# Reordered work at the layer boundaries of a two-block network kernel

## The reference

```python
mem_n = rmsnorm(mem, mem_norm_g)
for i in range(2):
    mem_k, mem_v = split(mem_n @ mem_w_kv[i])
    x = x + 0.5 * swiglu(rmsnorm(x, norm_g[i, 0]), ffn_w_up[i, 0], ffn_w_down[i, 0])
    h = rmsnorm(x, norm_g[i, 1])
    mix = pool_layer(h, ..., mem_k, mem_v) if i == 0 else diff_layer(h, ..., mem_k, mem_v)
    x = x + mix
    x = x + 0.5 * swiglu(rmsnorm(x, norm_g[i, 2]), ffn_w_up[i, 1], ffn_w_down[i, 1])
x = rmsnorm(x, final_norm_g)
```

```python
mod = silu(c) @ w_ada + b_ada            # 1024 x 6144 weights
x = x + g1 * hybrid_mixer(modulate(rms_norm(x), sh1, sc1), w_in, w_out, rel_bias)
x = x + g2 * peer_ffn(modulate(rms_norm(x), sh2, sc2), wq, subkeys, u_emb, v_emb)
```

## Time and profile before

| | us |
|---|---|
| three runs | 1996.73, 2003.67, 2005.41 |
| median | 2003.67 |
| span of the profiled execution | 1999.3 |
| PE busy in it | 1767.5 |
| DVE busy | 1275.6 |
| ACT busy | 795.6 |

### The profile page before, as it was taken

The page is one execution under the profiler, slowest core; times in us unless marked ns, Lnnn a source line. Parts: engine busy times, 40 slices in busy tenths (PEclk is TensorE's granted clock), DMA queues, the critical chain, the costliest instruction groups (busy, mean ns, idle before and its releaser), DMA issues.

```text
span 1999.3 us, 22974 instructions
## 1 busy us (share of the span) xinstructions
PE 1767.5 (88%) x8110; PEld 1301.8 (65%) x8110; DVE 1275.6 (64%) x2212; ACT 795.6 (40%) x1423; POOL 651.7 (33%) x602
## 2 busy tenths in 40 slices
PE   7999999999999999999999789759987787777786
PEld 6877898887888778978888788645533233333332
DVE  4567766665465556765654676478687888864554
ACT  5444435544354435575443456422222222321111
POOL 4453450144114451111444112023433334333330
PEclk9999999999999999999999799879999989899988
DMA  8999986799799989858999564378999999999995
GB/s 259 330 366 388 300 274 226 264 337 366 281 321 332 378 307 341 296 206 293 323 377 328 192 203 162 106 294 344 391 419 420 419 419 421 419 420 421 420 420 221
DMA packets 247275, 650.00 MB, mean 325 GB/s; under 512 B 14945, under 2 KB 156562, under 8 KB 214418
## 3 DMA queue, kind: packets, MB, share of 16 engines
q1 hardware_dynamic: 200210, 346.15, 50.4%
q0 software_dynamic: 46304, 301.52, 37.8%
q10 hardware_dynamic: 672, 1.18, 0.2%
HBM read 643.56 MB, written 139.48 MB: 392 GB/s over the span
## 4 chain that ended last, share of the span: by engine, by line
PE 44%; DMA 33%; POOL 9%; DVE 7%; issue 3%; ACT 3%; SPq 0%; ACTq 0%; DVEq 0%; POOLq 0%
DMA late_uv<-uv_rows,M 15%; DMA adaW<-in_w_ada 11%; PE P L1256 8%; DMA early_uv<-uv_rows,M 4%; PE P L719 3%; PE P L721 3%; PE P L720 3%; POOL adaW L556 3%; PE PX L802 3%; PE PX L804 3%; PE PX L803 3%; POOL adaW L557 2%; PE P L668 2%; POOL adaW L558 2%; PE P L669 2%
## 5 line engine op out<-in xcount | busy, mean ns | idle before, releaser
L1778 DVE TENSOR_TENSOR WL<-WR,WH 128x1024 fp32r<-128x1024 f32 (+1 forms) x246 | 323.8, 1357 | 203.4 <-ACT WH L1301 203.2
L1301 ACT ACTIVATE WH<-WR 128x1024 fp32r<-128x1024 f32 (+1 forms) x272 | 271.0, 1044 | 342.7 <-PE P L721 143.2
L1256 PE MATMUL P<-early_uv,M 128*128 128x512 f32 x576 | 280.8, 645 | 85.5 <-ACT M L1712 85.5
L802 PE MATMUL PX<-WH,hTh 128*128 128x512 f32 x704 | 280.6, 399 | 6.8 <-DVE WL L1786 4.5
L804 PE MATMUL PX<-WH,hTl 128*128 128x512 f32 x704 | 275.9, 392 | 0.0
L1256 PEld LDWEIGHTS P<-early_uv,M 128*128 128x128 f32 x576 | 115.6, 206 | 245.3 <-issue 141.0
L803 PE MATMUL PX<-WL,hTh 128*128 128x512 f32 x704 | 275.0, 391 | 0.0
L1256 PE MATMUL P<-late_uv,M 128*128 128x512 f32 x448 | 219.9, 648 | 60.3 <-ACT M L1712 60.3
L1793 DVE TENSOR_TENSOR WL<-WR,WH 128x1024 fp32r<-128x1024 f32 x128 | 179.2, 1440 | 136.9 <-ACT WH L1310 136.9
L653 POOL DMA_INDIRECT early_uv<-uv_rows,M x144 | 139.9, 972 | 302.2 <-PE P L1256 183.7
L2362 DVE CUSTOM_DVE_ANT_0 early_uv<-early_uv,PX 128x1024 f32<-128x1024 f32 x144 | 172.0, 1219 | 92.6 <-DMA early_uv<-uv_rows,M 92.2
(11 more groups left out here) (365 smaller groups left out, 3166.1 us busy)
## 6 DMA issues: line engine op xcount, KB each, us to landing
WR<-in_ffn_w_up SPq DMA_DIRECT2D x88, 1024.0 KB, 10.0
WR<-in_ffn_w_down SPq DMA_DIRECT2D x44, 1024.0 KB, 11.1
uv_rows<-in_peer_u SPq DMA_DIRECT2D x35, 1024.0 KB, 13.5
uv_rows<-in_peer_v SPq DMA_DIRECT2D x35, 1024.0 KB, 14.4
uv_rows<-in_peer_u SPq DMA_DIRECT2D x58, 512.0 KB, 9.6
uv_rows<-in_peer_v SPq DMA_DIRECT2D x58, 512.0 KB, 9.2
adaW<-in_w_ada POOLq DMA_DIRECT2D x48, 512.0 KB, 8.4
WR<-in_diff_w_in SPq DMA_DIRECT2D x14, 1024.0 KB, 13.0
```

The lines of the kernel that those rows point to most:

```text
L802: mm(o, xh, WH[:, u, w], start=(k == 0), stop=False)
L1256: last = mm(P[2 * t + q][:], diag[:, n % 2, i], rows_uv(n)[:, i, D + q * 512:D + q * 512 + 512], start=n % GROUPS == 0 and i == 0, stop=n ...
L1301: nc.scalar.activation(split_view(WH, U % 2, kind, part), raw(c % 2, kind, h, part), copy)\
L1778: tt(split_view(WL, U % 2, kind, part), raw(c % 2, kind, h, part), split_view(WH, U % 2, kind, part).bitcast(F32), ALU.subtract)\
```

## The change

No instruction is added or removed on PE and none on POOL and SP. The lists of PE, DVE and ACT are put in another order at these places:

- **Banks.** The first half of each down phase no longer waits for the low parts of tiles 9. It does banks P0, P1 and P2 for both k steps, waits (`bank3`) and then does both k steps of P3.
- **Ada.** The products of piece 5 move from step 1 of down01 to step 3, those of piece 7 from step 1 of down10 to step 3.
- **Memory norm.** DVE's 8 products are done 4 in step 5 and 4 in step 6, its low parts 2 in step 7 and 2 in step 8, ACT's high parts 2 in step 6 and 2 in step 7; the last window reciprocal moves from step 8 to step 9.
- **Updates.** In every layer's `add_update` the second update comes before the first part of the next WL. At pool_in the second part of that WL also comes before the last update, and the low parts of the norm come after it. At diff_in the third low part comes before the next half's WL, the transposes of pairs 2 and 3 come 4 products earlier on PE, and ACT's third high part comes before the first square.
- **pool_in.** ACT splits half 2 before it copies the row of scales.
- **Pool attention.** DVE's `mix_lo` comes after the attention result of the same step.
- **diff attention.** `subnorm_scale(0)` comes one step later on DVE, and PE's transposes for it come between the two k steps of the out half instead of ahead of it.

The diff:

```diff
--- before.py
+++ after.py
@@ -387,4 +387,4 @@
     ADA = {}
-    for i, (name, h) in enumerate([("down00", 0), ("down00", 1), ("pool_out", 0), ("pool_out", 2), ("down01", 0), ("down01", 1),
-                                   ("down10", 0), ("down10", 1), ("diff_in", 10), ("down11", 0), ("down11", 1), ("final", 0)]):
+    for i, (name, h) in enumerate([("down00", 0), ("down00", 1), ("pool_out", 0), ("pool_out", 2), ("down01", 0), ("down01", 3),
+                                   ("down10", 0), ("down10", 3), ("diff_in", 10), ("down11", 0), ("down11", 1), ("final", 0)]):
         ADA[(name, h)] = i
@@ -682,3 +682,3 @@
             for i, (b, k) in enumerate(order):
-                if i == KT and between:
+                if i == (KT if pieces is None else 4) and between:
                     between()
@@ -711,3 +711,3 @@
 
-        def rows_half(U, kt0, first, last_half, then=None):
+        def rows_half(U, kt0, first, last_half, then=None, middle=None, bank3=None):
 
@@ -731,2 +731,11 @@
                             last.then_inc(S["update_done"], 1)
+            elif bank3:
+                for kk in range(2):
+                    if kk:
+                        pe.wait_ge(S["lo_ready"], U + 1)
+                    for q, t in ((0, 0), (1, 0), (0, 1)):
+                        one(kk, q, t)
+                bank3()
+                for kk in range(2):
+                    last = one(kk, 1, 1)
             else:
@@ -734,2 +743,4 @@
                     if kk:
+                        if middle:
+                            middle()
                         pe.wait_ge(S["lo_ready"], U + 1)
@@ -873,6 +884,7 @@
             for v in range(p["n"]):
-                pe.wait_ge(S["act_lo"], c0 + (CHUNKS if v >= 2 else CHUNKS - 1))
+                pe.wait_ge(S["act_lo"], c0 + (CHUNKS if v >= 2 else CHUNKS - 1 if v else CHUNKS - 2))
                 if before_down:
                     before_down(v)
-                rows_half(p["U"] + v, 2 * v, v == 0, v == FT // 2 - 1, then)
+                rows_half(p["U"] + v, 2 * v, v == 0, v == FT // 2 - 1, then,
+                          bank3=None if v else lambda: pe.wait_ge(S["act_lo"], c0 + CHUNKS - 1))
                 if v == 0:
@@ -1059,3 +1071,3 @@
 
-        def out_half(v):
+        def out_half(v, middle=None):
             if v == 0:
@@ -1065,3 +1077,3 @@
                 pe.wait_ge(S["on_lo"], v - 1)
-            rows_half(phases["diff_out"]["U"] + v, 8 + 2 * v if v < 2 else 2 * v - 4, v == 0, v == 5, "up11")
+            rows_half(phases["diff_out"]["U"] + v, 8 + 2 * v if v < 2 else 2 * v - 4, v == 0, v == 5, "up11", middle)
 
@@ -1082,4 +1094,3 @@
             if i == 11:
-                subnorm(0)
-                out_half(1)
+                out_half(1, lambda: subnorm(0))
         attention(heads_of("mem1") + heads_of("diff"), dense_diff)
@@ -1334,4 +1345,8 @@
                 act.wait_ge(S["x_ready"], X_AFTER[X_FOR[name]])
-            square(0)
-            high(2)
+            if name == "diff_in":
+                high(2)
+                square(0)
+            else:
+                square(0)
+                high(2)
             high(3)
@@ -1491,5 +1506,6 @@
                 late_std("mem")
-            if v == 6:
-                act.wait_ge(S["half_used"], phases["down00"]["U"])
-                for q in range(4):
+            if v in (6, 7):
+                if v == 6:
+                    act.wait_ge(S["half_used"], phases["down00"]["U"])
+                for q in (2 * v - 12, 2 * v - 11):
                     act.wait_ge(S["hn_ready"], q + 1)
@@ -1502,4 +1518,4 @@
         p = phases["pool_in"]
-        scale_row(0)
         split(p["U"] + 2)
+        scale_row(0)
         split(p["U"] + 3)
@@ -1883,6 +1899,8 @@
             update(0, 0)
-            split_part(U, 0)
             update(0, 1)
+            split_part(U, 0)
             update(1, 0)
-            if after:
+            if after == "pool_in":
+                split_part(U, 1)
+            elif after:
                 late_lo(after, 0)
@@ -1890,3 +1908,7 @@
             update(1, 1)
-            split_part(U, 1)
+            if after == "pool_in":
+                late_lo(after, 0)
+                late_lo(after, 1)
+            else:
+                split_part(U, 1)
             if not after:
@@ -1894,4 +1916,8 @@
                 return
-            split_part(U + 1, 0)
-            late_lo(after, 2)
+            if after == "diff_in":
+                late_lo(after, 2)
+                split_part(U + 1, 0)
+            else:
+                split_part(U + 1, 0)
+                late_lo(after, 2)
             split_part(U + 1, 1)
@@ -2011,3 +2037,3 @@
 
-        def attention(units, dense):
+        def attention(units, dense, late=lambda i: None):
             def logits(x):
@@ -2072,2 +2098,3 @@
                     result(units[i - 1])
+                late(i)
 
@@ -2094,4 +2121,4 @@
         def mem_norm(v):
-            if v in (2, 3, 4, 8):
-                window_counts({2: 0, 3: 1, 4: 2, 8: 3}[v])
+            if v in (2, 3, 4, 9):
+                window_counts({2: 0, 3: 1, 4: 2, 9: 3}[v])
             if v == 1:
@@ -2101,3 +2128,4 @@
                 chain(nc.vector.reciprocal(rstd[:], rstd[:]))
-                for k in range(KT):
+            if v in (5, 6):
+                for k in range(4 * v - 20, 4 * v - 16):
                     last = stt(NT[:, k], memT[:, k], cols[:, G_MEM + k:G_MEM + k + 1], rstd[:], ALU.mult, ALU.mult)
@@ -2105,4 +2133,4 @@
                         last.then_inc(S["hn_ready"], 1)
-            if v == 7:
-                for q in range(4):
+            if v in (7, 8):
+                for q in (2 * v - 14, 2 * v - 13):
                     dve.wait_ge(S["hh_ready"], 4 * NORMS["mem"][2] + q + 1)
@@ -2159,6 +2187,9 @@
                 split(phases["group"]["U"] + i - 1)
-                mix_lo(g)
+
+        def late_pool(i):
+            if i >= 3:
+                mix_lo(2 * i - 6)
                 if i == 3:
-                    mix_lo(g + 1)
-        attention(heads_of("mem0"), dense_pool)
+                    mix_lo(1)
+        attention(heads_of("mem0"), dense_pool, late_pool)
         p = phases["pool_outx"]
@@ -2217,5 +2248,4 @@
                 half_diff(DIFF_SLOTS[i])
-            if i == 9:
-                subnorm_scale(0)
             if i == 10:
+                subnorm_scale(0)
                 split(phases["diff_out"]["U"] + 2)
```

6 lines of the change are left out of this document (3 added, 3 removed).

## The result

The changed kernel takes 1990.51 us (median of 12 runs, 1983.96 to 1998.38), the kernel before 2006.94 us (median of 12 runs beside them, 1995.86 to 2012.86). The ratio is 0.9919, 95% interval 0.9901 to 0.9937: some 16 us less. The forecast was 22 us less. So the direction held, and a quarter of the size is missing: by the interval the gain is 12.6 to 19.9 us, which does not reach 22. The profiled execution has a span of 1982.2 us, 17.1 less than the 1999.3 of before.

The account below looks back on a forecast made before the run. PE, busy 88% of the span, was taken to bound the kernel up to the gathers, with its waits and the low clock behind some of them as targets. The terms sum to 22.1 us; 2003.7 - 22.1 = 1981.6, say 1982, range 1973 to 1994.

Parts of the forecast that it names:

- rival A: In down01 and down10 the loads take back what the down phases gain: 11.4 us go, 1993 is left; chance 0.14.
- Down00, memory norm, updates: Down00 to kv0: waits on tiles 9, the memory norm and WL go, capped by loads; 5.5 us gained, between 2 and 7.
- pool_in: At pool_in, with WH ahead of the scales' copy, PE's wait of 2.66 and 1.7 of low clock go: 4.4 us.
- Pool attention: In the pool attention PE's wait at 327.11 shrinks and the next grows: 0.5 us lost (from -1 to +1.0).
- Down01 with piece 5: In down01 the wait on tiles 9 goes (3.8 us) and the wait for ada piece 5 with its low clock (2.8).
- Down10 with piece 7: In down10 the wait on tiles 9 goes (1.5 us) and the wait for ada piece 7 with its low clock (3.3).
- diff_in: At diff_in the 1.57 us wait goes, but PE then waits at the fourth piece: +0.2 us (from -1.7 to +3.6).
- diff attention: In the diff attention `subnorm_scale` no longer precedes what PE waited 1.37 us for; 0.3 returns later: +1.1 (0 to 1.4).
- Update order elsewhere: In the other layers WL's first part comes 0.7 us later, where PE needs it some 3 us later: 0.
- Behind it: In up11 and down11 any gain only lengthens PE's last ada wait, 10.06 us before and forecast at 11: 0.
- B: Rival: the ada chain's end is fixed, so all gain goes into the last ada wait of 10.06: 2003 us; chance 0.06.
- C: Rival: in up01, up10 and up11 loads don't move with PE, which waits at low clock: 6.5 slower, 2010 us; chance 0.05.

Follow-up runs that it names:

- the copies moved: The changed kernel with three pairs of uv copies (3 MB) moved from down00 to the first chunks of up01; ratio 0.9892 to the kernel before.

## Why the prediction was right or wrong

The direction was right, and so was the mechanism in down01 and down10, where most of the gain is made. The size was not: the sum of 22.1 is 16.4 by the medians, outside the +-5 that the forecast gave itself, 17.1 in the profile and 12.0 in a second one. That 1990.51 us lies in the range of 1973 to 1994 is partly luck: its high end was drawn to take in rival A, which did not happen. Of the signs on record, POOL's last chain starts 15.1 us earlier and not some 22, and the lead near the gathers is 16.0, just over the 15 below which the prediction called itself wrong. By its own terms, with the two profiles' leads:

- *Down00, memory norm, updates, 5.5 (2 to 7)*: 5.1 and 2.8. The loads do limit it. The place differs: PE waited not at the fifth half but ahead of the third, for the ada piece (3.41), and the clock was low for 6.8 us, not 3.4. The piece's sums had been ready since 143.7; its products also wait until DVE has added the last piece's, and that stands behind a WL that waits for its load, as the timelines of ACT and DVE show:

```profile
158.45 2.00 ACT L1312 ACTIVATE WH<-WR 128x1024 fp32r<-128x1024 f32 x2 [5.51 <-DMA WR<-in_ffn_w_down]
159.54 2.36 DVE L1794 TENSOR_TENSOR WL<-WR,WH 128x1024 fp32r<-128x1024 f32 x2 [5.87 <-ACT WH L1312]
...
161.81 0.15 DVE L1870 TENSOR_TENSOR modc<-PX,badac 128x4 f32<-128x4 f32 x1
```

  For the update order 1.2 was forecast; in the run with the memory norm alone the order of the first two updates leaves PE a wait of 4.99 us, but what it is worth isn't shown.
- *pool_in, 4.4*: the wait and its low clock went, as forecast, but the term is mis-sized: from kv0's first half to pool_in's fifth the lead grew by 2.3 in both profiles, half of it. Where the rest went was not found.
- *Pool attention, -0.5*: -1.4 and -1.2. The edit's own cost is 0.2 us of waiting; whether it is the 0.5 forecast isn't shown. The collision of POOL's sums with WL, for which the prediction had no term, makes a wait of 1.7.
- *Down01 with piece 5, 3.8 + 2.8 = 6.6*: 7.3 and 7.4. *Down10 with piece 7, 1.5 + 3.3 = 4.8*: 5.9 and 4.4. The sums are near, the split isn't: the banks alone gave nothing, the pieces alone 4.4 and 2.4. The two are stages of one chain of waits, and what each is worth depends on the other.
- *diff_in, +0.2 (-1.7 to +3.6)*: -5.7 and -3.2. This is the step that failed. It had seen that the high parts begin by ACT's list in any case and that PE would wait for a low part. But it had no term for the load ahead of ACT's list: the first WH waits for it, it took 10.0 us from issue to landing instead of 7.8, so of a lead of 19.2 only 17.3 came through, and PE's first wait of 2.84 us and the low clock follow. And it took DVE's work from there as the same pieces in another order. A piece that is moved ahead on DVE brings its own wait with it: 2.26 us for the third high part, spent with two WL parts behind, and 0.7 where PE's first wait was short. By the ten profiles that order costs about 1.0 us; a loss of 3 us and more comes only with a first wait of 2.47 us or more, under the old order too. Nor had it a term for the collision with POOL's sums there, though the 3.45 us of WL that it read in the earlier trace rows contained one. Why the load lands late is open.
- *diff attention, +1.1*: +1.6 and +1.5 at diff_out's third half (the second loses it again before up11, where a low stretch begins at 869.8). *Update order elsewhere, 0*: nothing seen.
- *Behind it, 0*: +0.9 and +3.9 up to out2. The last ada wait was forecast at 11 and was 6.03, because POOL's chain was 4.3 us shorter; 2.2 of that went into the next wait, for the norm. That wait hides the ada piece: the path there is in2's load, ACT's four WH parts, a table load and the squares, as the timeline of ACT shows.

```profile
1083.30 3.90 ACT L1312 ACTIVATE WH<-WR 128x1024 fp32r<-128x1024 f32 x4 [7.79 <-DMA WR<-in_w_in]
1087.21 1.28 ACT L1595 ACT_TABLE_LOAD   x1
...
1092.57 1.06 ACT L1599 ACTIVATE M<-M 128x1024 f32<-128x1024 f32 x1 [1.78 <-DVE M L2266]
```

Of the rivals, A (the loads take back what down01 and down10 gain) fell: both kept their gain. Its mechanism acts one stage on, at diff_in, where 1.9 us stayed with a late load and more behind it. B fell: the ada chain moved with PE by 15.1 us. It was nearer the truth than its 0.06, though: in three runs the lead fell by 4 to 6 us where the chain was long. C fell: in the changed kernel's two profiles no lead was lost inside an up phase. A stretch at low clock was priced at 1.7 us. In diff_in it was less: 17 matmuls in 3.5 us where full clock does 27 in 3.27, so 3.4 us at the low clock lose 1.4. In down00 17 stand against 31 in windows of 6.6 us, some of them lost to the wait itself.

## What to carry to other kernels

When an instruction is moved ahead on an in-order engine, carry its wait along: ask when its input is ready at the new place, and what is now queued behind it. Neighbouring waits on the busiest engine are links of one chain, so price them together, and expect nothing from one taken away alone. Before blaming the edit for a loss, look at the same place in every other profile that holds the edit: here three of five had no loss. And look for whatever runs at its own pace beside the list that is being reordered (a load stream, a slow side engine): a lead moves the list against it, and the collisions change place.

## What the runs showed of the hardware that was not expected

- A WL part on DVE (128x1024) takes 1.2 us with POOL idle (in the 14 traces, up to 1100 us, none of those that overlap no POOL operation is over 1.23) and about 2.4 beside POOL's additions (two parts: 2.35 against 4.76), while POOL's own 128x512 addition takes 2.14 us beside WL, where 1.29 was its time at the same place before. The Trainium skill (SBUF — State Buffer, "SBUF: two separate sides") has the two engines take a shared pair of ports by an exclusive lock for a whole instruction, the loser waiting, where the DVE operation has two inputs in SBUF, as WL has, and POOL's reads SBUF; by that rule both would lose time where they meet, and the trace agrees, with 2.41 us more on DVE's two parts and 0.85 more on POOL's addition.
- Two profiles of one program differ by up to 2.3 us of lead in the early stages, where loads are at 420 GB/s and one or another lands later, by 3.5 at the end of down10 and by 5 us in the span, so a term under 2 us needs two profiles or a run that isolates it.
- Between 140 and 1030 us the low clock comes in stretches of 3.4 and 6.8 us, and the length of a wait does not tell which. It is 3.4 us behind waits of 1.10 to 3.50 us in the kernel before and at the 4.99 of the run with the memory norm alone; it is 6.8 us at the 3.41 in down00 and at the 4.91 and 5.07 of the run with the banks alone, where the clock falls while PE still waits. A wait need not bring it: none stands behind the 2.81 us with all of diff_in put back, and behind the 1.58 us at the end of the pool attention there is none in the changed kernel and one of 3.4 us with the copies moved.
